# Weight sums of a seven-product MLP moved from four accumulating DMAs to two VectorE sums and two accumulating DMAs, with x parked in DRAM

## What is computed

```python
x, c                                  # (1, 512, 1024), (1, 1024)
for i in range(2):
    sh_m, sc_m, gt_m, sh_f, sc_f, gt_f = split(silu(c) @ ada_w[i] + ada_b[i], 6)
    h = rms_norm(x, norm_g[i, 0]) * (1 + sc_m) + sh_m
    y = pool_mixer(h) if i == 0 else short_conv_mixer(h)
    x = x + gt_m * rms_norm(y, norm_g[i, 1])
    h = rms_norm(x, norm_g[i, 2]) * (1 + sc_f) + sh_f
    y = square(relu(h @ ffn_w1[i])) @ ffn_w2[i]       # 1024 -> 4096 -> 1024
    x = x + gt_f * rms_norm(y, norm_g[i, 3])
```

## Time and profile before

| | us |
|---|---|
| median of 3 runs | 1015.38 (1014.44 to 1019.2) |
| the profiled execution, device time | 1020.67 |
| its span, first to last instruction | 1018.9 |
| PE busy | 943.7 (93%) |
| DVE busy | 606.8 (60%) |
| ACT busy | 409.8 (40%) |
| POOL busy | 67.1 (7%) |
| DMA read / written | 160.66 MB / 2.13 MB |

### The profile page before, as it was taken

How to read it: one execution, slowest core, us unless ns; L and a number is a source line. 1 busy time by engine, 2 the same in 40 slices (tenths; PEclk the granted TensorE clock), 3 DMA queues, 4 the chain that set the end, 5 groups by cost and what they waited for, 6 DMA issues and landing times.

```text
span 1018.9 us, 11390 instructions
## 1 busy us (share of the span) xinstructions
PE 943.7 (93%) x4647; PEld 773.1 (76%) x4647; DVE 606.8 (60%) x622; ACT 409.8 (40%) x497; POOL 67.1 (7%) x94
## 2 busy tenths in 40 slices
PE   8889959996999699999999999997999699979997
PEld 6658848884887588889888888985888488858886
DVE  6776476446745667687667545756644662565444
ACT  6544543334335223354332233455243433532432
POOL 3001010021002100000101000001000100000000
PEclk8999989997999799999999999999899799979999
DMA  9996377546654874604755531374654652475301
GB/s 299 329 353 236 93 145 206 208 109 120 230 172 103 165 267 167 222 7 165 230 188 194 184 104 42 108 220 85 190 182 100 114 181 83 98 152 163 123 19 65
DMA packets 90092, 163.53 MB, mean 160 GB/s; under 512 B 4238, under 2 KB 34034, under 8 KB 90040
## 3 DMA queue, kind: packets, MB, share of 16 engines
q1 hardware_dynamic: 75208, 133.23, 38.8%
q0 software_dynamic: 14832, 29.57, 15.8%
HBM read 160.66 MB, written 2.13 MB: 160 GB/s over the span
## 4 chain that ended last, share of the span: by engine, by line
PE 72%; DMA 12%; DVE 7%; ACT 4%; issue 4%; POOL 1%; SPq 0%; DVEq 0%; ACTq 0%; POOLq 0%
PE ps L574 23%; PE ps L575 23%; PE ps L576 23%; DMA raw<-in_ffn_w_dram 9%; DVE w_parts L1280 2%; ACT w_parts L1002 2%; DMA raw<-in_ada_w_dram 2%; PE ps L777 1%; DMA xs<-in_x_dram 1%; DVE ops_lo L1322 1%; PE ps L668 1%; DMA rows_dram<-fin 0%; PE ps L855 0%; POOL g_four L1829 0%; ACT work L1012 0%
## 5 line engine op out<-in xcount | busy, mean ns | idle before, releaser
L1280 DVE TENSOR_TENSOR w_parts<-raw,w_parts 128x2048 fp32r<-128x2048 f32 x99 | 226.8, 2290 | 195.8 <-ACT w_parts L1002 195.7
L1002 ACT ACTIVATE w_parts<-raw 128x2048 fp32r<-128x2048 f32 x99 | 188.8, 1911 | 356.1 <-PE ps L576 244.0
L574 PE MATMUL ps<-in_hi,w_parts 128*128 128x512 f32 (+1 forms) x784 | 290.0, 370 | 0.9 <-DVE in_lo L1427 0.5
L576 PE MATMUL ps<-in_hi,w_parts 128*128 128x512 f32 (+1 forms) x784 | 288.1, 367 | 0.0
L575 PE MATMUL ps<-in_lo,w_parts 128*128 128x512 f32 (+1 forms) x784 | 288.0, 367 | 0.0
L574 PEld LDWEIGHTS ps<-in_hi,w_parts 128*128 128x128 f32 x784 | 147.7, 188 | 29.5 <-issue 3.3
L576 PEld LDWEIGHTS ps<-in_hi,w_parts 128*128 128x128 f32 x784 | 147.7, 188 | 24.4
L575 PEld LDWEIGHTS ps<-in_lo,w_parts 128*128 128x128 f32 x784 | 147.8, 189 | 24.0
L574 PE MATMUL ps<-w_parts,ops_hi 128*128 128x512 f32 x288 | 119.8, 416 | 46.0 <-DVE y L1336 26.6
L575 PE MATMUL ps<-w_parts,ops_hi 128*128 128x512 f32 x288 | 118.0, 410 | 0.0
L574 PEld LDWEIGHTS ps<-w_parts,ops_hi 128*128 128x128 f32 x288 | 58.1, 202 | 61.2 <-issue 48.8
(11 more groups left out here) (184 smaller groups left out, 923.7 us busy)
## 6 DMA issues: line engine op xcount, KB each, us to landing
raw<-in_ffn_w_dram SPq DMA_DIRECT2D x58, 1024.0 KB, 5.3
ada_raw<-in_ada_w_dram SPq DMA_DIRECT2D x56, 512.0 KB, 6.1
raw<-in_ffn_w_dram POOLq DMA_DIRECT2D x24, 1024.0 KB, 8.7
raw<-in_conv_in_w_dram SPq DMA_DIRECT2D x16, 512.0 KB, 5.1
raw<-in_ada_w_dram SPq DMA_DIRECT2D x4, 1024.0 KB, 11.6
ada_sum<-in_ada_w_dram SPq DMA_DIRECT2D x4, 1024.0 KB, 12.2
win<-in_ada_w_dram SPq DMA_DIRECT2D x4, 1024.0 KB, 12.1
raw<-in_conv_in_w_dram SPq DMA_DIRECT2D x4, 1024.0 KB, 5.5
```

Of the source, the lines that this page charges most:

```text
L574: nc.tensor.matmul(o, hi, b_hi, start=start, stop=False, skip_group_check=on)
L576: return nc.tensor.matmul(o, lo, b_hi, start=False, stop=stop, skip_group_check=on)
L1002: nc.scalar.activation(w_hi[:, u % W_SLOTS, :], raw[:, u % RAW_SLOTS, :], ACT.Copy).then_inc(w_hi_ready, 1)
L1280: nc.vector.tensor_tensor(w_lo[:, u % W_SLOTS, :], raw[:, u % RAW_SLOTS, :], w_hi[:, u % W_SLOTS, :].bitcast(F32), ALU.subtract).then_inc( ...
```

## The change

`xs` is stored to a DRAM tensor at the start of each MLP (`save_x`), its place holds two weight blocks during the three seven-product quarters, and it is loaded back in the last quarter (`load_x`). N's and S's weights are made by VectorE in that place (`make_parts`), during the `ffn_w1` units ahead of the stage; R's and A22's still by accumulating DMA, A22's onto N's block in the place of x. The two raw slots then go round over the other units alone (`ring`). S's operand is made earlier, with an own place for its high part (`s_hi`, over `work` and `cu`), Q's operand low part comes one step earlier, and in the first quarter of a layer ScalarE reads the eight new banks (`read_new`) instead of VectorE. In POOL's list the rows move behind R's DMA, and the clearing of `cu`'s edges moves behind the first MLP.

```diff
-PART = ((0, 0, False), (1, 0, False), (0, 1, True), (1, 1, False), (1, 1, True), (0, 1, True), (1, 0, True))
+PART = ((0, 0), (1, 0), (0, 1), (1, 1), None, None, (1, 0))
+X_PART = ((0, 1), (1, 1))
+OP_ORDER = (A11, S, A12, R, Q_, N, A22)
...
+        x_dram = nc.dram_tensor("x_dram", (T, D), F32, kind="Internal").ap()
+        x_part = [xs[:, 2 * i:2 * i + 2, :].rearrange("p j d -> p (j d)") for i in range(2)]
...
+        ring = [u for u in range(UNITS) if not seven_of(u) or seven_of(u)[2] < N]
+        def raw_slot(u):
+            return ring.index(u) % RAW_SLOTS
+        def slot_before(u):
+            return ring[ring.index(u) - RAW_SLOTS]
+        def raw_of(u):
+            if seven_of(u) and seven_of(u)[2] >= N:
+                return x_part[1 if seven_of(u)[2] == S else 0]
+            return raw[:, raw_slot(u), :]
...
+            def save_x(layer):
+                if layer == 0:
+                    sp.wait_ge(x1_norm, NT)
+                    sp.wait_ge(x1_sq, NT)
+                else:
+                    sp.wait_ge(h_scaled, tile_value(2, NT - 1))
+                    sp.wait_ge(x_sq, tile_value(2, NT - 1))
+                sp.dma_start(x_dram.rearrange("(j p) d -> p j d", p=P), xs[:, :, :]).then_inc(x_saved, 16)
+            def load_x_parts(layer, q):
+                if q == 0:
+                    sp.wait_ge(x_saved, 16 * (layer + 1))
+                for i in (1, 0):
+                    if q > 0:
+                        sp.wait_ge(w_lo_ready, quarter_unit(layer, q - 1) + 4 + (A22 if i == 0 else S) + 1)
+                    sp.dma_start(x_part[i].rearrange("p (k n) -> p k n", k=UK), w2_part(layer, q, *X_PART[i])).then_inc(x_part_in[i], 16)
+            def load_x(layer):
+                sp.wait_ge(w_lo_ready, quarter_unit(layer, SEVEN_QUARTERS))
+                sp.dma_start(xs[:, :, :], x_dram.rearrange("(j p) d -> p j d", p=P)).then_inc(x_back, 16)
...
             for u in range(4, UNITS):
                 if not seven_of(u):
                     load(u)
-                elif not added(u):
+                elif seven_of(u)[2] in (A11, A12, Q_):
                     load_seven(u)
+                for layer in (0, 1):
+                    if u == FFN_U[layer] + 4:
+                        save_x(layer)
+                        load_x_parts(layer, 0)
+                    for q in (1, 2):
+                        if u == quarter_unit(layer, q) + 1:
+                            load_x_parts(layer, q)
+                    if u == quarter_unit(layer, SEVEN_QUARTERS) + 2:
+                        load_x(layer)
...
+            def read_new(layer, s, t):
+                act.wait_ge(bank_done, seven_done(layer, 0, s, t))
+                i, h, sign = TARGET[s]
+                nc.scalar.activation(y_tok[:, 2 * i + t, half(h)], seven_bank(layer, 0, s, t), ACT.Copy, scale=float(sign)).then_inc(y_new, 1)
...
                 operand_hi(layer, q, N)
+                if q == 0:
+                    read_new(layer, A11, 0)
+                    read_new(layer, A11, 1)
                 split_hi(u + 4)
-                operand_hi(layer, q, S)
                 operand_hi(layer, q, A22)
-                for s in range(5, SEVEN + 2):
-                    split_hi(u + s)
+                split_hi(u + 5)
+                if q == 0:
+                    read_new(layer, R, 0)
+                    read_new(layer, R, 1)
+                    read_new(layer, Q_, 0)
+                    read_new(layer, Q_, 1)
+                split_hi(u + 6)
+                split_hi(u + 7)
+                split_hi(u + 8)
+                if q == 0:
+                    read_new(layer, A22, 0)
+                    read_new(layer, A22, 1)
...
             def read_seven(layer, q, s, t):
+                if q == 0 and s in TARGET_NEW:
+                    return
...
+            def make_parts(layer, q):
+                i = stage(layer, q)
+                dve.wait_ge(x_part_in[0], 16 * (i + 1))
+                dve.wait_ge(x_part_in[1], 16 * (i + 1))
+                nc.vector.tensor_tensor(x_part[1], x_part[1], x_part[0], ALU.add).then_inc(part_made, 1)
+                u = quarter_unit(layer, q) + 4
+                dve.wait_ge(part_made, 2 * i + 1)
+                wait_raw(dve, u)
+                nc.vector.tensor_tensor(x_part[0], x_part[1], raw_of(u), ALU.add).then_inc(part_made, 1)
...
                 operand_lo(layer, q, R)
+                operand_lo(layer, q, Q_)
+                step(u + 1)
                 read_seven(layer, q, A11, 0)
                 read_seven(layer, q, A11, 1)
-                step(u + 1)
-                operand_lo(layer, q, Q_)
+                step(u + 2)
+                operand_lo(layer, q, N)
                 read_seven(layer, q, A12, 0)
                 read_seven(layer, q, A12, 1)
-                step(u + 2)
-                operand_lo(layer, q, N)
                 read_seven(layer, q, R, 0)
                 read_seven(layer, q, R, 1)
                 step(u + 3)
+                operand_lo(layer, q, A22)
                 read_seven(layer, q, Q_, 0)
                 read_seven(layer, q, Q_, 1)
-                operand_lo(layer, q, S)
                 read_seven(layer, q, N, 0)
+                read_seven(layer, q, N, 1)
                 step(u + 4)
-                read_seven(layer, q, N, 1)
-                operand_lo(layer, q, A22)
                 read_seven(layer, q, S, 0)
...
                         if j == 1:
+                            operand_sum(layer, q, S)
                             operand_lo(layer, q, A11)
-                            operand_sum(layer, q, S)
+                            operand_lo(layer, q, S)
+                        if j == 2:
+                            make_parts(layer, q)
...
+            def add_part(layer, q, s):
+                u = quarter_unit(layer, q) + 4 + s
+                if s == R:
+                    pool.wait_ge(w_lo_ready, u - 1)
+                    pool.wait_ge(part_made, 2 * stage(layer, q) + 2)
+                else:
+                    pool.wait_ge(w_lo_ready, u - 1)
+                pool.dma_start(raw_cols(u), seven_part(u), accum_op=ALU.add).then_inc(r_part_in if s == R else last_part_in, 16)
...
+            for q in range(SEVEN_QUARTERS):
+                add_part(0, q, R)
+                if q > 0:
+                    send_row(q - 1)
+                if q == 1:
+                    spread_row(0)
+                add_part(0, q, A22)
             send_row(2)
...
+            for q in range(SEVEN_QUARTERS):
+                add_part(1, q, R)
+                if q == 1:
+                    send_row(6)
+                    spread_row(6)
+                add_part(1, q, A22)
```

More of the change, by code:

```diff
@@ L175, in trunk @@
         work = sb("work", [P, 2, T])
+        with ExitStack() as early:
+            s_hi = sb("s_hi", [P, UK, 2 * P], F32R, early)
         cu = sb("cu", [P, 2, T + 2])
@@ L208, in trunk @@
         raw_in = [sem(f"raw_in{s}") for s in range(RAW_SLOTS)]
-        part_in = [sem(f"part_in{s}") for s in range(RAW_SLOTS)]
+        r_part_in, last_part_in, part_made = sem("r_part_in"), sem("last_part_in"), sem("part_made")
+        x_part_in = [sem(f"x_part_in{s}") for s in range(2)]
+        x_saved, x_back = sem("x_saved"), sem("x_back")
         pre_in = [sem(f"pre_in{s}") for s in range(9)]
@@ L243, in trunk, with w2_part @@
         block = ctx.enter_context(nc.Block())
[L245 to L262, removed]
         def raw_cols(u, cols=slice(0, UN)):
-            return raw[:, u % RAW_SLOTS, :].rearrange("p (k n) -> p k n", k=UK)[:, :, cols]
+            return raw_of(u).rearrange("p (k n) -> p k n", k=UK)[:, :, cols]
         def w_rows(w):
             return w.rearrange("(k p) n -> p k n", p=P)
+        def w2_part(layer, q, kk, h):
+            return w_rows(ffn_w2[layer, q * QF + kk * UK * P:q * QF + (kk + 1) * UK * P, h * UN:(h + 1) * UN])
         def seven_part(u):
             layer, q, s = seven_of(u)
-            kk, h, _ = PART[s]
-            return w_rows(ffn_w2[layer, q * QF + kk * UK * P:q * QF + (kk + 1) * UK * P, h * UN:(h + 1) * UN])
+            return w2_part(layer, q, *PART[s])
         def ada_rows(layer):
@@ L371, in seven_bank, with added, wait_raw, raw_value @@
             return ps[:, banks(p)[t if CHAIN[s] == "x" else 2 + t], :]
+        ring = [u for u in range(UNITS) if not seven_of(u) or seven_of(u)[2] < N]
[3 more added lines that the diff above has]
+            return ring[ring.index(u) - RAW_SLOTS]
+        def added(u):
+            return seven_of(u) is not None and seven_of(u)[2] in (R, A22)
+        def raw_of(u):
+            if seven_of(u) and seven_of(u)[2] >= N:
+                return x_part[1 if seven_of(u)[2] == S else 0]
+            return raw[:, raw_slot(u), :]
+        def wait_raw(eng, u):
+            if seven_of(u) and seven_of(u)[2] in (R, N, S, A22):
+                layer, q, s = seven_of(u)
+                i = stage(layer, q)
+                if s == R:
```

(28 more changed lines are left out.)

62 lines of the change are left out of this document (27 added, 35 removed).

## The result

The kernel became faster: 983.95 us in the median of 4 runs (982.06 to 984.63) against 1017.29 us of the kernel before in its runs (1014.44 to 1020.07). The ratio is 0.967 (95% interval 0.963 to 0.971). The forecast was 978.4 us in a range of 963 to 996; it was reckoned as 1015.4 us less 37.0. Measured on the median of 1017.29 us the gain is 33.3 us, and on the 1015.4 us it would be 31.4.

A forecast was written before the change was run, and what follows sets the result against it. Bound by TensorE's waits and slow matmuls in six seven-product stages (78.5 us lost). Stages 2, 3, 5, 6 -32.6, stage 4 -3.6, stage 1 -0.8: -37.0 from 1015.4 gives 978.4 us, range 963 to 996.

The forecast's parts named there:

- Q's wait does not go, it is set by VectorE's order: In stages 2, 3, 5 and 6, Q still waits 3.2 us for VectorE's read of R, starting at 19.5 instead of 16.3.
- Slow clock behind it: After Q's idle 3.2 us, matmuls run slowly and cost 1.7 us per stage, taken from the row with 3.62 us idle.
- R's DMA in time: Issued at t = -7.5 behind both weight sums, R's accumulating DMA lands at 1.2 (8.7 us), so PE does not wait.
- The bound of 4.3: R's DMA may land as late as t = 4.3 us after A11's first matmul without harm.
- Store of x: Storing x before the two block loads takes 9 us, between bounds of 7.0 and 17; in stage 4 R starts 2.2 late.
- Stage 1: First quarter of the first MLP: A12 waits 7.3 us behind VectorE's sums; stage end 175.2 instead of 176.0, -0.8 us.
- Covers set at nothing: x loaded back in the last quarter, and SP standing until A22's low part delaying later block loads, each cost 0 us.
- Rival B: x traffic and the later R not covered, store 17 us: 1000 us at worst, 989 half-way; chance 0.18.
- D: No change: something else holds Q, so the sums do not relieve VectorE; 1015 us; chance 0.05.
- E: Slower: R's add, tied behind both sums, becomes each stage's long wait; 1027 us if it lands 20 us after issue; chance 0.05.
- C: The short waits cost no clock and x is in by 673, R in time: 963 us; chance 0.17.

The follow-up runs named there:

- the first experiment: Kernel after with R's banks read right behind N's low part on VectorE and ahead of S's high part on ScalarE: 961.27 us, ratio 0.945 to the kernel before.
- the doubled sums: Kernel after with two more 128x2048 VectorE operations ahead of the weight sums of stages 2, 3, 5 and 6: 997.08 us (single run).
- The early sums: Stage 1's two weight sums made ahead of S's operand sum, on top of the early store: 949.73 us, ratio 0.936 to the kernel before.
- the early store: The first experiment with x stored behind unit 3's load in layer 0 and ahead of A11's load in layer 1: 955.56 us, ratio 0.942 to the kernel before.

## Why the prediction was right

- **Q's wait does not go, it is set by VectorE's order.** Predicted 3.2 us, measured 3.0 in stages 2, 3, 5 and 6, with the starts in VectorE's list in stage 3 within 0.1 us of the forecast from low part of Q on; the first experiment shows the cause. This was the term on which the forecast hung: who had taken the DMA as the only limit would have said 40 us a stage or less.
- **Slow clock behind it, 1.7 us for each stage**, from the row nearest in idle time. This term was mis-sized: it was 3.0, 3.1, 0.2 and 3.0 us (length less 38.1 and the wait of 3.0) for the same idle time, so no stage took the 1.7. In the row of 3.62 us the clock stood at 0.50 for 3.4 us of matmuls, here for 5.8 to 6.2. The trace of the kernel before held the larger size too: in its sixth stage the wait of 7.02 us cost 40.91 - 38.1 = 2.8 us of clock. That the mean is 2.3 and the four stages came to 173.7 us instead of 172.0 is partly luck: with the clock down in all four it would have been some 176.5.
- **R's DMA in time.** It landed after 9.5 to 10.1 us in these stages, not 8.7, and still by t = 3.0; PE did not wait. The 8.7 us were the median of all 24 accumulating DMAs; R's own six in the kernel before had taken 8.6 to 13.0 us, four of them 10.3 or more. The bound of 4.3 was about right, as the doubled sums showed.
- **Store of x, 9 us taken, 12.0 measured** in the fourth stage. That is the mis-sized term there: the stage took 46.0 us instead of 44.9, with 3.1 us at R instead of 2.2. When the store was issued ahead of A11's load, with no load issued until it had landed, it took 6.6 us. That is near the 6.8 that the formula of the Trainium skill ("DMA: Bandwidth & Descriptors", "Anatomy of one DMA") gives, though the page fits it to DMAs that GpSimd issues and SP issues this one. Right behind a 1 MB load (6.3 us to landing) it took the 12.0.
- **Stage 1** was to take 53.0 and took 53.5 us: 7.2 us at A12 (predicted 7.3), 1.1 at R, 2.6 at Q. The early sums confirm that VectorE's list was its cause.
- **Covers set at nothing** (x coming back, SP standing until A22's low part, ScalarE's reads): no wait at the first block of a quarter, and none for x at the boundaries; from the first MLP on PE has no wait above 0.5 us outside the stages. VectorE's busy time rose by 16.4 us (606.8 to 623.2), forecast 16.
- **The rivals.** Rival B's size for the store came a little over a third of the way (12.0, between 9 and 17), its late R only in the doubled sums. D and E did not happen. C's gains needed other edits: no clock loss in stages 2, 3, 5 and 6 came with R's banks read first, R of stage 4 in time came with the early store, and together they gave more than C had, because the wait at Q itself shrank too.

In sum -33.7 us in the stages instead of -37.0: 1.7 in the four stages (2.5 more of clock, 0.8 less of wait), 1.1 in stage 4, mostly the store, and 0.5 in stage 1. The median, 983.95 us against the 978.4 forecast, holds 1.9 us more that are no part of the change: the kernel before, measured once more, had its median at 1017.29 us instead of 1015.38.

Open: why the clock fell in three of four stages with the same wait; the change without POOL's new order, of which only the reverse (the order in the kernel before) was run; and how much of the gain needs the parking, because the kernel before was not run with N's two reads ahead of A22's low part.

## What to carry to other kernels

When a chain of DMAs is shortened, walk the engine that stood at its end: if it works in order, what it does after its wait may be the next limit, and moving R's reads a few places up was worth 23 us here. Before giving buffers, try the orders alone, and all of them; here two gave 28 us, about as much as the whole change (33), while the change and the new read order together gave 55. A transfer that several others must wait for is better issued ahead of the load beside it: here the store then took 6.6 instead of 12.0 us.

## What the runs showed of the hardware

One idle time gave different clocks. The stretches of 4 us behind the four Q waits of 2.99, 2.99, 3.00 and 2.98 us in the kernel after:

```profile
237.00:241.00 4.00, 4.00 (x10) 0.50 1.04 189
325.30:329.30 4.00, 4.00 (x10) 0.50 1.04 182
780.10:784.10 4.00, 4.00 (x18) 1.00 1.07 188
865.00:869.00 4.00, 4.00 (x10) 0.50 1.09 198
```

Three ran at 1.2 GHz and one at 2.4, so a wait of 3 us costs here 3.2 or 6.1 us. It is not the place: with the first quarter's reads back on VectorE, the same four stages had the same waits (2.98 to 3.00 us) and lost 1.8, 3.1, 3.1 and 1.9 us to the clock (PE busy less 38.1), the third of them the one that had lost 0.2. Behind the wait of 3.14 us at R in stage 4 of the kernel after the clock stayed at 1.00 too, up to the next wait. Behind the waits of 0.66 us of the first experiment it stayed at 1.00 in every one of the four stages.

A store of 2 MB took 12.0 us right behind a 1 MB load, and 6.6 us where the load ahead of it was issued 4.4 us earlier and none behind it (the early store in layer 1). The early store in layer 0, behind other loads of 1 MB, took 13.3 us. An accumulating DMA of 1 MB onto a raw slot (R's) took 10.0 us in the median, each time with a plain load issued 1.6 to 2.4 us behind it, and 8.6 onto the place of x (A22's). The place is not the likely reason: A22's DMAs of the kernel before, also onto a raw slot, took 8.4 to 8.8 us.
